# Second block of a two-block network: softmax table ahead of the maximum, last state product amid the attention projection, merged transposes between tiles, last down rows by tile

## What is computed

```python
    h = rms_norm(x, norm_mix_w[l])
    x = x + hybrid_mixer(h, ...)
    h = rms_norm(x, norm_ffn_w[l])
    x = x + conv_glu_ffn(h, ffn_w_up[l], ffn_conv_w[l], ffn_conv_b[l], ffn_w_down[l])

def hybrid_mixer(h, ...):
    proj = h @ w_in          # q, k, v, index heads, z, xbc, dt, two gates
    a = dsa_attention(q, k, v, q_idx, k_idx, w_idx)      # softmax over the keys that an index selects
    b = mamba2_branch(z, xbc, dt, ...)                   # chunked state scan, gated by silu(z), group norm
    merged = sigmoid(g_attn) * (a @ w_proj_attn) + sigmoid(g_ssd) * (b @ w_proj_ssd)
    return merged @ w_out

def conv_glu_ffn(h, w_up, conv_w, conv_b, w_down):
    u = causal_dwconv(h @ w_up, conv_w, conv_b)
    gate, val = u[..., :FFN_DIM], u[..., FFN_DIM:]
    return (jax.nn.silu(gate) * val) @ w_down
```

## Time and profile before

| | us |
|---|---|
| median of 3 runs | 2164.5 |
| lowest and highest | 2161.58, 2165.36 |
| the profiled execution | 2165.75 |
| its span in the profile | 2163.9 |
| TensorE busy in it | 1954.8 |
| VectorE, ScalarE, GpSimd busy | 1379.5, 1041.5, 1055.0 |

### The profile page before, as it was taken

The page is one execution under the profiler, slowest core; times in us unless marked ns, Lnnn a source line. Parts: engine busy times, 40 slices in busy tenths (PEclk is TensorE's granted clock), DMA queues, the critical chain, the costliest instruction groups (busy, mean ns, idle before and its releaser), DMA issues.

```text
span 2163.9 us, 26303 instructions
## 1 busy us (share of the span) xinstructions
PE 1954.8 (90%) x9022; PEld 1429.6 (66%) x9022; DVE 1379.5 (64%) x2864; ACT 1041.5 (48%) x1957; POOL 1055.0 (49%) x856
## 2 busy tenths in 40 slices
PE   7999988888777788778999999999999999999998
PEld 3967767633233333233699777888879977778887
DVE  5668765676666676665377743288854775326887
ACT  4514545321221122221545687476664568846665
POOL 1723677654444444433687567810048865683000
PEclk9999999999999999989999999999999999999999
DMA  9523864899999999999555454555545534455653
GB/s 346 172 74 132 265 247 154 350 421 421 421 421 421 422 421 421 421 421 402 196 177 166 130 174 144 177 172 199 184 159 178 179 128 163 151 183 166 201 189 108
DMA packets 111733, 534.27 MB, mean 247 GB/s; under 512 B 12528, under 2 KB 12912, under 8 KB 78320
## 3 DMA queue, kind: packets, MB, share of 16 engines
q1 hardware_dynamic: 68112, 248.18, 34.2%
q0 software_dynamic: 38720, 275.96, 31.0%
q10 hardware_dynamic: 4768, 8.46, 1.3%
HBM read 531.43 MB, written 1.11 MB: 246 GB/s over the span
## 4 chain that ended last, share of the span: by engine, by line
PE 60%; DMA 22%; ACT 6%; DVE 5%; issue 3%; POOL 3%; ACTq 0%; SPq 0%; DVEq 0%; POOLq 0%
PE psum L903 58%; DMA pair_rows<-in_peer_uv,arena 10%; DMA arena<-in_peer_uv,arena 7%; DMA wring<-in_peer_uv,arena 3%; PE psum L982 2%; POOL w_lo L2983 2%; ACT w_hi L1542 2%; POOL w_lo L2981 1%; ACT arena L1553 1%; DVE arena L2926 1%; DVE w_lo L2027 0%; ACT arena L1917 0%; DMA wring<-in_w_in_hy 0%; ACT a_parts L1549 0%; ACT arena L1788 0%
## 5 line engine op out<-in xcount | busy, mean ns | idle before, releaser
L903 PE MATMUL psum<-w_hi,a_parts 128*128 128x512 f32 (+1 forms) x2112 | 674.4, 394 | 24.1 <-POOL w_lo L2983 12.2
L2981 POOL TENSOR_TENSOR w_lo<-wring,w_hi 128x512 fp32r<-128x512 f32 (+1 forms) x288 | 386.1, 1341 | 497.3 <-ACT w_hi L1542 481.4
L1542 ACT ACTIVATE w_hi<-wring 128x1024 fp32r<-128x1024 f32 (+1 forms) x414 | 431.6, 1053 | 282.6 <-PE psum L903 247.2
L903 PE MATMUL psum<-a_parts,w_hi 128*128 128x256 f32 (+1 forms) x1984 | 474.6, 325 | 3.3 <-DVE a_parts L2080 1.6
L903 PEld LDWEIGHTS psum<-w_hi,a_parts 128*128 128x128 f32 x2112 | 396.8, 189 | 121.0 <-POOL w_lo L2983 16.8
L903 PE MATMUL psum<-w_lo,a_parts 128*128 128x512 f32 (+1 forms) x1056 | 409.6, 388 | 0.0
L2983 POOL TENSOR_TENSOR w_lo<-wring,w_hi 128x512 fp32r<-128x512 f32 (+1 forms) x288 | 402.8, 1399 | 0.0
L903 PE MATMUL psum<-arena 128*128 128x512 f32 (+7 forms) x1148 | 327.6, 447 | 69.6 <-ACT arena L1788 46.5
L903 PE MATMUL psum<-a_parts,w_lo 128*128 128x256 f32 x1312 | 362.2, 283 | 0.0
L903 PEld LDWEIGHTS psum<-a_parts,w_hi 128*128 128x128 f32 x1984 | 328.7, 192 | 36.4 <-issue 4.4
L903 PEld LDWEIGHTS psum<-arena 128*128 128x128 f32 (+2 forms) x1148 | 182.4, 196 | 197.7 <-issue 116.8
(11 more groups left out here) (266 smaller groups left out, 2086.5 us busy)
## 6 DMA issues: line engine op xcount, KB each, us to landing
wring<-in_w_up SPq DMA_DIRECT2D x88, 512.0 KB, 4.2
wring<-in_w_xbc SPq DMA_DIRECT2D x48, 512.0 KB, 4.2
wring<-in_w_dn SPq DMA_DIRECT2D x44, 512.0 KB, 3.9
wring<-in_w_adaT SPq DMA_DIRECT2D x32, 512.0 KB, 4.4
wring<-in_w_qkv SPq DMA_DIRECT2D x32, 512.0 KB, 3.6
wring<-in_w_z SPq DMA_DIRECT2D x32, 512.0 KB, 3.7
wring<-in_w_g SPq DMA_DIRECT2D x32, 512.0 KB, 3.8
wring<-in_w_ps SPq DMA_DIRECT2D x32, 512.0 KB, 3.8
```

Source lines behind the costliest of these rows:

```text
L903: mm = lambda o, a, b, start, stop: nc.tensor.matmul(o, a, b, start=start, stop=stop, skip_group_check=True)
L1542: a.reaches(A(w_hi[:, n % SPLIT_RING, 0:width], wring[:, c % RING, 0:width], ACT.Copy), hi_ready, n + 1)
L2981: nc.gpsimd.tensor_tensor(w_lo[:, r, 0:half], wring[:, c % RING, 0:half], w_hi[:, r, 0:half].bitcast(F32), ALU.subtract)
```

## The change

1. `exponentials`: for the second tile the split of the last `w2_z` chunk and a dummy Exp of one column (which brings the table load with it) stand ahead of the wait for the maximum. Behind it, only gate chunk 0 is split ahead of `acsT` and only chunk 1 ahead of the `z` reads by these lines (the stream's own order puts chunk 2 there as well).
2. `ssd_out(7)` stands half-way through the first call on `w2_pa`. ScalarE's split of `w2_pa` chunk 5 stands behind the squares of six pieces instead of eight, and the squares wait for the bank of `ssd_out(6)`, whose input they overwrite.
3. The second `merged_turned` stands between the two token tiles of the second chunk of `w2_o` (`amid`).
4. The last two down chunks are awaited one by one: the earlier one for outputs 0 and 2, the last one for 0 and 2, then both for 1 and for 3.

```diff
+DOWN_END = [(n, k) for k in (FT - 2, FT - 1) for n in (0, 2)] + [(n, k) for n in (1, 3) for k in (FT - 2, FT - 1)]
...
                 for n, g in enumerate(outs):
+                    if amid and kp == k_parts // 2 - 1 and n == 1:
+                        amid()
                     last = kp == k_parts - 1 and not last_by_tile
...
-            ssd_out(SSD_G * TT - 1)
             for t in range(TT * KVH):
                 wait_read(pe, L + "o", t)
-            for c in range(2):
-                columns_of_rows("w2_pa", l, [(L + "pa", 2 * c), (L + "pa", 2 * c + 1)], [AT_AT] * 2)
+            columns_of_rows("w2_pa", l, [(L + "pa", 0), (L + "pa", 1)], [AT_AT] * 2, early=True,
+                            before=lambda: ssd_out(SSD_G * TT - 1))
+            columns_of_rows("w2_pa", l, [(L + "pa", 2), (L + "pa", 3)], [AT_AT] * 2)
...
             columns_of_rows("w2_o", l, [(L + "wo", 0), (L + "wo", 1)], [0, 0], early=True,
-                            before=lambda: merged_turned(L + "mT", merged2, 1, 4 + 2 * l),
+                            amid=lambda: merged_turned(L + "mT", merged2, 1, 4 + 2 * l),
                             ready=lambda k: wait_read(pe, L + "mT", k))
...
-                    pe.wait_ge(S("glu_ready"), FT * l + FT)
-                    last_two = [take("w2_dn", l), take("w2_dn", l)]
-                    for n in DOWN_ORDER:
-                        for k, w in zip((FT - 2, FT - 1), last_two):
-                            m = rows_mm(down[n], GLU_AT + k % GLU_RING, 1, n % 2, w, 512, False, k == FT - 1,
-                                        at=512 * (n // 2))
+                    last_two = []
+                    for n, k in DOWN_END:
+                        if k - (FT - 2) == len(last_two):
+                            pe.wait_ge(S("glu_ready"), FT * l + k + 1)
+                            last_two.append(take("w2_dn", l))
+                        m = rows_mm(down[n], GLU_AT + k % GLU_RING, 1, n % 2, last_two[k - (FT - 2)], 512, False,
+                                    k == FT - 1, at=512 * (n // 2))
...
             def exponentials(t, first):
                 n_keys = P * (t + 1)
-                act.wait_ge(S("max2"), TT * l + t + 1)
                 if t:
                     weights_upto(act, "w2_z", l, first + 1)
+                    a.done(A(lnw[:, 0:1], K("epscol"), ACT.Exp))
+                act.wait_ge(S("max2"), TT * l + t + 1)
                 for h in range(H2):
-                    if h in (2, 5):
+                    if h in (2, 5) and not t:
                         weights_upto(act, "w2_z", l, first + (h == 5))
...
-            weights_upto(act, "w2_g", l, 1)
+            weights_upto(act, "w2_g", l, 0)
             read_out(L + "acsT", 0, acsT, bank(L + "acsT", 0)[0:64, 0:P])
...
-            weights_upto(act, "w2_g", l, 2)
+            weights_upto(act, "w2_g", l, 1)
             z_out(6)
...
             weights_upto(act, "w2_pa", l, 4)
+            act.wait_ge(psum_filled, turn[(L + "y", SSD_G * TT - 2)] + 1)
             for i in range(SSD_G * TT):
                 g, t = i // TT, i % TT
+                if i == SSD_G * TT - 2:
+                    weights_upto(act, "w2_pa", l, 5)
...
-            weights_upto(act, "w2_pa", l, 5)
```

More of the change, by code:

```diff
@@ L926, in columns_of_rows @@
         def columns_of_rows(name, l, outs, srcs, k_parts=4, nk=2, before=None, early=False,
-                            ready=None, later=None, last_by_tile=False):
+                            ready=None, later=None, last_by_tile=False, amid=None):
             o = [open_(*g, early=early) for g in outs]
@@ L1508, in _ @@
                 if c == FT // 2:
[L1509 to L1517 removed]
+                    last_two = []
[5 more added lines that the diff above has]
+                                    k == FT - 1, at=512 * (n // 2))
+                        if (n, k) == (3, FT - 2):
+                            m.then_inc(weights_used, 1)
+                        if k == FT - 1:
+                            close(m)
                     break
```

3 lines of the change are left out of this document (removed).

## The result

| | us |
|---|---|
| kernel before, median of 6 runs (lowest to highest) | 2164.39 (2161.58 to 2169.52) |
| changed kernel, median of 6 runs (lowest to highest) | 2153.09 (2149.33 to 2157.83) |
| changed to before | 0.9948, 95% interval 0.9935 to 0.996 |
| the profiled execution of the changed kernel | 2157.83 |
| its span | 2156.0 |

The change brings 11.3 us, just over half of the 21.6 that were forecast; 2153.09 lies above the range of 2139 to 2151. The sign was right, the size was not.

What follows compares the result with a forecast made beforehand. TensorE, busy nine tenths of the span, was taken as the bound: its work plus gaps. Gains of 5.3 + 12.0 + 1.8 + 2.5 = 21.6 us gave a median of 2142.9, range 2139 to 2151, forecast chance 0.65.

Steps and rivals of the forecast that it cites:

- Part 1: Softmax, both layers: copy and table load fill ScalarE's idle time, removing TensorE's 2.37 us stop before turning probabilities; gain 5.3.
- the 0.68 left over: Amid the probability transposes: TensorE's 0.68 us wait for a bank ScalarE frees by reading `z` was to stay.
- Part 2: Attention projection, both layers: no wait for VectorE's decay product, full clock, no wait at the seventh chunk; gain 12.0 us.
- up to 0.15: Attention projection: TensorE might wait this many us for the low half of the second chunk.
- Part 3: Merged transposes between the tiles: six matmuls cover TensorE's 0.72 us wait, in layer 1 also 0.42; gain 1.8 in all.
- Part 4: Last down rows, both layers: two tiles of the earlier chunk cover waits of 1.35 and 1.36 us; gain 2.5.
- rival (a): TensorE's clock falls all the same, not bound to the wait; 7.7 us stay, time 2150.6; chance 0.14.
- (d): Nothing arrives: another wait of each place takes over, time 2164.5 us; chance 0.04.
- (e): Slower: the new break in the projection leaves TensorE at low clock through dense work, 2213 us; chance 0.03.
- (b): GpSimd becomes the bound of the projection, so part 2's waits stay: 2147.9 us; chance 0.08.
- (c): The state loop swallows part 1, its decay rows coming by a DMA round trip keeping its own time: 2148.2; chance 0.06.
- square root 6 us sooner relative to the first projection matmul: Sign for part 2: ScalarE's square root, formerly behind all squares and a held weight copy, comes 6 us sooner.

Runs made afterwards that it cites:

- the run without the dummy Exp: The changed kernel with only the dummy Exp taken out, the chunk copy still ahead of the maximum: 2150.27 us in one execution.
- held: The changed kernel plus a GpSimd wait holding the low half of the last z chunk until VectorE has the second tile's maximum: 2148.88 us, ratio 0.9922.
- part 4 alone: The kernel before with only part 4 of the change: 2164.07 us, ratio 0.9991.
- two or three holds: Changed kernel, GpSimd waits: last z chunk's low half behind the maximum, next layer's second (and third) qkv chunk's behind first (second) tile's scaling: 2146.84 (2146.89) us.
- parts 2 and 1 tried alone: The kernel before with only part 2, 2154.92 us; with only part 1, 2165.96; with part 1 and GpSimd's wait for the maximum, 2160.67.
- part 1 alone: The kernel before with only part 1 of the change, no wait added on GpSimd: 2165.96 us, ratio 1.0004.

## Why the prediction was wrong

**Part 1, the step that failed** is the sentence "The chunk's low half on GpSimd is earlier too, not later." It is true, and it was priced at nothing because earlier looked harmless. Earlier put it beside two of VectorE's last steps ahead of the decay sums. These steps were in the trace of before, at 0.23 and 0.19, and so were their neighbours beside GpSimd's other pieces, 64 columns in 1.2 us (L2110 at 1205.15, 1.21 long). The move was followed through ScalarE's queue and to GpSimd's, but not to what GpSimd's instruction does to the engine beside it. The kernel before even has a hold of the kind that was missing, in `weights_low`: one `w2_up` chunk waits there for `tile_scaled`. Of the 8.05 us between the forecast gain of 5.3 and the measured loss of 2.75, the stop is some 3.9 and the clock's fall behind it 4.2, by the run without the dummy Exp. The rest of the part was right: held, it gave 2.34 and 3.07 for the forecast 2.3 and 3.0, with the 0.68 left over in place and the second layer's slow transposes gone with the stop.

The Trainium skill (SBUF — State Buffer, "Who interferes with whom") has a rule for this: a VectorE instruction with two SBUF inputs contends with a GpSimd instruction that reads SBUF, and one in a two-port mode contends with GpSimd as well; there, whoever issues first gets the shared ports for the whole instruction, and the other blocks. The rows agree, down to the ends that fall together within 0.1 us; whether the steps with a single input (`TENSOR_SCALAR`) were in such a mode no run shows. Weighed in the prediction, it would have spoken against this edit.

**Part 2, right, 0.5 too high.** 11.5 for 12.0, each layer 0.25 short. Its mechanism is as told: no wait for the decay product, full clock, no wait at the seventh chunk. The 0.25 fits the delay at the second chunk, for which the prediction allowed "up to 0.15" and which took 0.3. (VectorE's steps on the last product "will end near 1314.7" is 1314.9 by the prediction's own terms; nothing hung on it.) What the prediction did not say in its range is that over half of the term is the clock's and doesn't always fall due: in the kernel with part 4 alone, whose code is that of before at this place, the product behind the same 1.70 stop took 2.91 instead of the 4.73 of the earlier trace rows, and the stage 94.21 instead of 97.40. The part is worth 2.7 to 5.9 a layer, by the execution.

**Part 3, right, 0.5 too low.** 2.3 for 1.8. The bracketed idle time of 0.72 in the earlier trace rows counts from the modelled end of the last transpose. The eight transposes took

```profile
1390.45 1.03 PE L982 MATMUL psum<-consts,arena 128*128 128x128 f32 x8
```

before, and where nothing waits the next matmul starts 0.79 behind such a row (1388.43 to 1389.22 in the changed kernel):

```profile
1388.43 1.03 PE L985 MATMUL psum<-consts,arena 128*128 128x128 f32 x8
1389.22 0.48 PE L904 MATMUL psum<-w_hi,a_parts 128*128 128x512 f32 x1
```

So the stop cost 1392.21 - 1390.45 - 0.79 = 0.97, not 0.72, and 0.95 was gained. This stop cost 0.25 us more than its bracket says.

**Part 4, right in layer 1, wrong in layer 0.** The end gained 1.32 for 1.25. At the border the sentence "The banks close in the old order, the first 0.8 us earlier and the others 1.4" was followed only to "what then sets the norm is the second bank". Counted from the feed-forward part's turned rows, the norm's scaling moved from 185.21 to 184.07 us, to a place where GpSimd works without a break, and grew from 1.33 to 2.38. It gave back 1.1 there and 1.1 more behind, by the clock. It is part 1's miss once more: here VectorE moved beside GpSimd, there GpSimd beside VectorE.

**The clock.** Of what made it fall, the prediction had half. The forecast was that it falls behind stops and not by itself; rival (a) said it falls all the same. With two or three holds, where no stop is longer than 1.5 us, none of the second block was lost to it. Rivals (d) and (e) fall with the whole time, and (b) and (c) by parts 2 and 1 tried alone. But that the fall goes with the stop holds one way only. The fourteen profiles of the table's kernels hold 35 stops of 1.7 to 2.4 us in the second block: behind 10 of them 3.0 to 3.4 us were lost, behind 20 1.4 to 1.7, behind 5 nothing (first layer, is one; the kernel without the dummy Exp has two). Nor does a fall need so long a stop: with part 1 alone, 1.7 us were lost at the border behind two stops of 0.88 and 0.87 (1599.59 and 1601.56), where the kernel before has 0.86 and 0.87 and lost nothing. So a new stop cost its length and up to 3.2 on top in these stages (97.40 against 94.21), which was nowhere in the sum's range. In the changed kernel the loss is as large as before, 8.2 for 8.3: what part 2 took away, the two new kinds of stop brought back.

**The signs for the reader.** Of the signs named ahead, "no idle over 0.3 us before the probabilities are turned" and "the copy and table load of ScalarE ahead of the maximum" both came true while the part lost time; the one that told was "Wrong if a clock of 0.50 appears at a new place". Of part 2's signs, "square root 6 us sooner relative to the first projection matmul" did not come as it is worded: 14.07 us behind that matmul before (1323.46 against 1309.39) and 13.58 in the changed kernel (1322.52 against 1308.94). Counted from the first gate matmul it comes 6.1 sooner, which is what the working had. The projection with its product took 24.95 for "24 to 24.5". A sign should be the length of the whole stage, not the absence of the old wait.

## What to carry to other kernels

When an edit lets one engine start earlier, follow the work that it triggers down to the steps of other engines that will then run beside it: here steps of 0.2 us took 1.2, as long as the neighbour's whole instruction. A transfer or split with slack should be held behind the neighbour's critical steps rather than started when its input is ready; one wait for `max2` on GpSimd turned part 1 from nothing into 5.4 us. And hold it only as far as the slack goes: the second hold brought 1.5 us, and the third gave 0.7 of it back at the border.

## What the runs showed of the hardware

- Small VectorE steps of 64 columns took 0.19 to 0.23 us alone, and 1.16 and 1.22 while GpSimd subtracted 512 columns from SBUF (1.26 us); each ended within 0.1 us of GpSimd's instruction. Two scalings of 512 columns took 0.88 alone and 2.36 to 2.47 beside GpSimd.
- TensorE's granted clock fell to its lower level behind 30 of 35 stops of 1.7 to 2.4 us, and once behind two of 0.9, but not behind each: the same 2.00 us stop at the same place was followed by a loss of 3.3 us (changed kernel, twice), 1.7 (part 1 alone) and 0 (without the dummy Exp). The Trainium skill (TensorE: Matmul & The Clock Gate, "Why this matters for your kernels") warns of idle gaps longer than any of these; here the shorter ones were enough.
- A table load of 1.28 us was followed by the next instruction 0.01 or 0.02 us later wherever that waited for nothing (1213.47 + 1.28 and 1214.76), so no kernel here shows a drain beside it.
- The table load does not wait with the Exp that needs it: without the dummy Exp it ran at 1210.88, and its Exp, held by VectorE's maximum, at 1219.93.
